# Two encoder layers on one core: earlier DMA slots, past keys turned ahead of the mixer, retention steps regrouped, and a GpSimd power on 128x320 numbers

## What is computed

```python
def _layer(x, l, P, past_k, past_v, s_gla0, s_ret0):
    x = x + 0.5 * _rms_norm(_swiglu(_rms_norm(x, ...), ...), ...)
    m, k_rows, v_rows, s_gla, s_ret = _mixer(_rms_norm(x, ...), ...)
    x = x + _rms_norm(m, ...)
    x = x + 0.5 * _rms_norm(_swiglu(_rms_norm(x, ...), ...), ...)

def _mixer(h, ...):
    z = h @ w_in                                    # low rank, then 26 tiles of 128 columns
    o_a = _rms_norm(_gla_chunked(...)) * silu(gr)    # 4 heads of 64: y tiles 0, 1
    o_d = _rms_norm(_diff_attention(q, [past_k | k], [past_v | v], ...)) * (1 - lam)  # y tiles 2 to 5
    o_r = _layer_norm(_retention_chunked(...)) * silu(rg)    # 4 heads of 64: y tiles 6, 7
    return concatenate([o_a, o_d, o_r]) @ w_out      # norm: y * 1/sqrt(mean(y*y) + eps), per head
```

## Time and profile before

| | us |
|---|---|
| median of 3 runs | 1334.51 (1334.36 to 1334.72) |
| the profiled execution | 1334.34 |
| its span on the core | 1332.6 |
| PE busy | 1315.2 |
| DVE, ACT, POOL busy | 813.3, 634.2, 131.6 |

### The profile page before, as it was taken

How to read it: one execution, slowest core, us unless ns; L and a number is a source line. 1 busy time by engine, 2 the same in 40 slices (tenths; PEclk the granted TensorE clock), 3 DMA queues, 4 the chain that set the end, 5 groups by cost and what they waited for, 6 DMA issues and landing times.

```text
span 1332.6 us, 24615 instructions
## 1 busy us (share of the span) xinstructions
PE 1315.2 (99%) x9508; PEld 1287.2 (97%) x9508; DVE 813.3 (61%) x1263; ACT 634.2 (48%) x1015; POOL 131.6 (10%) x176
## 2 busy tenths in 40 slices
PE   9999999999999999999999999999999999999998
PEld 7999999999999999999999999999999999999998
DVE  6756544687776855554385555437876777556432
ACT  6444434564466644443464443437535575444333
POOL 1000000451010200000030000005500130000000
PEclk9999999999999999999999999999999999999999
DMA  7555554563344454545545544455533355555552
GB/s 210 163 165 161 168 162 144 140 160 93 87 132 127 131 154 143 156 139 151 152 127 146 153 144 146 145 141 160 139 88 90 94 142 169 147 150 147 144 147 66
DMA packets 352027, 187.41 MB, mean 141 GB/s; under 512 B 9016, under 2 KB 348788, under 8 KB 351960
## 3 DMA queue, kind: packets, MB, share of 16 engines
q1 hardware_dynamic: 348376, 177.78, 47.4%
q0 software_dynamic: 2800, 7.85, 1.8%
q10 hardware_dynamic: 784, 0.86, 0.2%
HBM read 180.82 MB, written 4.33 MB: 139 GB/s over the span
## 4 chain that ended last, share of the span: by engine, by line
PE 91%; DVE 4%; POOL 1%; ACT 1%; DVEq 1%; issue 1%; DMA 0%; ACTq 0%; SPq 0%; POOLq 0%
PE ps L716 27%; PE ps L718 26%; PE ps L717 26%; PE ps L745 1%; PE ps L749 1%; PE ps L752 1%; DVE w_l L569 1%; POOL x L577 1%; PE ps L991 1%; PE ps L967 0%; DVEq L1728 0%; PE ps L1076 0%; DVE tiny L1729 0%; PE ps L1055 0%; PE ps L881 0%
## 5 line engine op out<-in xcount | busy, mean ns | idle before, releaser
L716 PE MATMUL ps<-xn_l,w_h 128*128 128x320 f32 x1704 | 536.3, 315 | 2.4 <-DVE w_l L569 2.4
L718 PE MATMUL ps<-xn_h,w_h 128*128 128x320 f32 x1704 | 526.9, 309 | 0.0
L717 PE MATMUL ps<-xn_h,w_l 128*128 128x320 f32 x1704 | 526.8, 309 | 0.0
L569 DVE TENSOR_TENSOR w_l<-raw,w_h 128x1024 fp32r<-128x1024 f32 (+1 forms) x336 | 401.1, 1197 | 158.6 <-ACT w_h L557 158.3
L557 ACT ACTIVATE w_h<-raw 128x1024 fp32r<-128x1024 f32 (+1 forms) x336 | 346.4, 1034 | 210.2 <-DMA raw<-in_ffn_w_down_dram 127.5
L716 PEld LDWEIGHTS ps<-xn_l,w_h 128*128 128x128 f32 x1704 | 321.0, 188 | 6.9 <-issue 3.9
L717 PEld LDWEIGHTS ps<-xn_h,w_l 128*128 128x128 f32 x1704 | 321.0, 188 | 1.0
L718 PEld LDWEIGHTS ps<-xn_h,w_h 128*128 128x128 f32 x1704 | 320.8, 188 | 0.0
L716 PE MATMUL ps<-hid_l,w_h 128*128 128x320 f32 x704 | 217.4, 309 | 0.0
L718 PE MATMUL ps<-hid_h,w_h 128*128 128x320 f32 x704 | 217.4, 309 | 0.0
L717 PE MATMUL ps<-hid_h,w_l 128*128 128x320 f32 x704 | 217.4, 309 | 0.0
(11 more groups left out here) (303 smaller groups left out, 1256.5 us busy)
## 6 DMA issues: line engine op xcount, KB each, us to landing
raw<-in_ffn_w_up_dram SPq DMA_DIRECT2D x172, 512.0 KB, 3.9
raw<-in_ffn_w_down_dram SPq DMA_DIRECT2D x64, 448.0 KB, 3.6
raw<-in_w_in_dram SPq DMA_DIRECT2D x52, 512.0 KB, 3.8
raw<-in_ffn_w_down_dram SPq DMA_DIRECT2D x32, 512.0 KB, 4.0
raw<-in_w_out_dram SPq DMA_DIRECT2D x16, 512.0 KB, 4.1
const<-in_tables_dram POOLq DMA_DIRECT2D x8, 288.0 KB, 4.4
raw<-in_ffn_w_up_dram SPq DMA_DIRECT2D x8, 256.0 KB, 6.6
y<-z SPq DMA_DIRECT2D x16, 80.0 KB, 2.2
```

The source lines that it names most:

```text
L569: dve.tensor_tensor(w_l[s][:, 0:cols], raw[s][:, 0:cols], w_h[s][:, 0:cols], ALU.subtract).then_inc(w_lo, 1)
L716: pe.matmul(out, w_h[s][:, w], xl, start=first, stop=False)
L717: pe.matmul(out, w_l[s][:, w], xh, start=False, stop=False)
L718: return pe.matmul(out, w_h[s][:, w], xh, start=False, stop=last)
```

## The change

1. `first_step` reports the slot of blocks k-1 and k used after each odd k, not all four at the end. The sum of squares of x is multiplied ahead of tiles 4 and 5, not between them. On DVE `other_params` and `lambda_sums` come two steps later.
2. The past keys have a buffer of their own in the upper half of `xn_l`, are loaded by POOL after the last up tile, turned on PE in the border in place of two of the four fillers, and copied by ACT after its squares. DVE waits for the turn before `xn_l` block 4. The step `past` is gone from the schedule.
3. The low-rank tile and the next one are multiplied together for blocks 4 to 7: all that needs `xn_h` first, then all that needs `xn_l`.
4. `ret_o 1` and `ret_mu 1` are each moved ahead of the attention steps of their place; the squares of y tiles 0, 1, 6 and 7 are a step `squares g` one tile earlier.
5. Group a's root: DVE adds eps (128x320, from PSUM), POOL raises the 128x320 numbers to -0.5, and a new step `halves`, one tile later, splits them on DVE. ACT's Sqrt is gone.
6. The first `spread` writes bank 3, so it waits for ACT's `tok7`, and the second for `att_max10`, not for `att_max11`.

```diff
 def first_step(k):
                 for t in range(OPENING):
                     mm = pe.matmul(ps[:, t, 0:T], w_h[s][:, first_block(t, k)], xn_l[:, k, :], start=False, stop=k == KD - 1)
-                    if k == KD - 1:
-                        mm.then_inc(w_used, 1)
+                if k % 2:
+                    mm.then_inc(w_used, 1)
...
+                pe.wait_ge(x_sum, 1)
+                pe.matmul(ps_stat[:, 0:T], sq_2[:, 0:P], ssum[:, :], start=True, stop=True).then_inc(x_stat, 1)
                 for t in range(OPENING, OPENING + 2):
...
-                        stat_x(0, 0)
...
+            def low_rank_and_next(l, n):
+                rest = range(KD // 2, KD)
+                block = lambda w, t, k: w[slot(l, U_MIX + t)][:, k * P:(k + 1) * P]
+                for k in rest:
+                    pe.wait_ge(xn_hi, (l * 4 + n) * KD + k + 1)
+                    pe.matmul(ps[:, 0, 0:T], block(w_h, 0, k), xn_h[:, k, :], start=False, stop=False)
+                for k in rest:
+                    pe.matmul(ps[:, 1, 0:T], block(w_h, 1, k), xn_h[:, k, :], start=False, stop=False)
+                    pe.matmul(ps[:, 1, 0:T], block(w_l, 1, k), xn_h[:, k, :], start=False, stop=False)
+                for t in range(2):
+                    for k in rest:
+                        if t == 0:
+                            pe.wait_ge(xn_lo, (l * 4 + n) * KD + k + 1)
+                        mm = pe.matmul(ps[:, t, 0:T], block(w_h, t, k), xn_l[:, k, :], start=False, stop=k == KD - 1)
+                    mm.then_inc(w_used, 1)
...
                     spread(l, norm // 2)
-                    keep_busy(4)
+                    if norm == 0:
+                        turn_past_keys(l)
+                        keep_busy(2)
+                    else:
+                        keep_busy(4)
...
-    + [("att_t", 1), ("att_s", 3), ("att_a", 2), ("ret_o", 1)] + P8[18][:1] + [("att_o", 1), ("ret_mu", 0)] + P8[18][1:]
-    + [("att_t", 2), ("att_s", 4), ("att_a", 3), ("ret_mu", 1)] + P8[19][:1] + [("att_o", 2), ("tok", 1)] + P8[19][1:]
+    + [("ret_o", 1), ("att_t", 1), ("att_s", 3), ("att_a", 2)] + P8[18][:1] + [("att_o", 1), ("ret_mu", 0)] + P8[18][1:]
+    + [("ret_mu", 1), ("att_t", 2), ("att_s", 4), ("att_a", 3)] + P8[19][:1] + [("att_o", 2), ("tok", 1)] + P8[19][1:]
...
     + [("att_t", 7), ("att_s", 9), ("att_a", 8), ("stat", "a"), ("root", "a")] + P8[24][:1] + [("att_o", 7), ("tok", 7)] + P8[24][1:]
-    + [("att_t", 8), ("att_s", 10), ("att_a", 9)] + P8[25][:1] + [("att_o", 8), ("squares", "b")] + P8[25][1:]
+    + [("att_t", 8), ("att_s", 10), ("att_a", 9)] + P8[25][:1] + [("att_o", 8), ("squares", "b"), ("halves", "a")] + P8[25][1:]
...
-                    elif kind == "root" and n != "a":
+                    elif kind == "root":
+                        dst, src = (inv_a, var_a) if n == "a" else (inv_h[:, STAT_OF[n] - 4, :], var_h[:, STAT_OF[n] - 4, :])
                         after(pool, l, "dve", f"var_{n}")
...
+                        power = minus_half[:, 0:1].broadcast_to([P, T]) if n == "a" else minus_half[:, :]
+                        mark("pool", pool.tensor_tensor(dst, src, power, ALU.pow), f"inv_{n}")
...
+                elif kind == "halves":
+                    after(dve, l, "pool", "inv_a")
+                    dve.tensor_copy(inv_2[:, :], inv_a)
```

More of the change, by code:

```diff
@@ L174, in milestones @@
         elif kind == "root":
[L175 to L180, removed]
+            dve.append(f"var_{n}")
+            pool.append(f"inv_{n}")
+        elif kind == "halves":
+            dve.append("inv_2")
         elif kind == "gates":
@@ L191 @@
 READER = {"tok": ("act", "tok"), "ret_kt": ("act", "ret_kt"), "ketok": ("act", "ketok"), "ret_s": ("dve", "ret_s"),
-          "ret_state": ("dve", "ret_state"), "ret_o": ("dve", "ret_o"), "ret_mu": ("dve", "ret_xc"), "stat": ("act", "sqrt_")}
+          "ret_state": ("dve", "ret_state"), "ret_o": ("dve", "ret_o"), "ret_mu": ("dve", "ret_xc"), "stat": ("dve", "var_")}
 SHARED = [(kind, "" if not arg else arg[0]) for kind, *arg in SCHEDULE
@@ L656, in _ @@
                 pool.memset(near[:, :, :], 0.0)
+                after(pool, l, "pe", "kct1")
+                then_pass(pool)
+                for b, t in ((0, 0), (1, 64), (2, 0)):
+                    i = pool.memset(scores[:, :, b, t:t + 64], 0.0)
+                i.then_inc(mem_set, 1)
                 for kind, *arg in SCHEDULE:
                     n = arg[0] if arg else None
[L659 to L665, removed]
+                    if kind == "weight":
                         qk(l, n)
@@ L718, in product @@
                 return pe.matmul(out, w_h[s][:, w], xh, start=False, stop=last)
-            def low_rank_part(s, bank, k0, k1):
-                for k in range(k0, k1):
-                    w = w_h[s][:, k * P:(k + 1) * P]
-                    pe.matmul(ps[:, bank, 0:T], w, xn_l[:, k, :], start=k == 0, stop=False)
-                    mm = pe.matmul(ps[:, bank, 0:T], w, xn_h[:, k, :], start=False, stop=k == KD - 1)
-                if k1 == KD:
-                    mm.then_inc(w_used, 1)
             def tile_part(s, bank, k0, k1, order=range(KD), xh=xn_h, xl=xn_l):
@@ L759, in opening @@
                     opening_step(l, u0, n, i)
-                for t in range(OPENING):
+                if u0 == U_MIX:
+                    low_rank_and_next(l, n)
+                for t in range(2 if u0 == U_MIX else 0, OPENING):
                     if t == OPENING - 1:
@@ L845, in ffn, with turn_past_keys @@
                     spread(l, norm // 2)
-                    keep_busy(4)
+                    if norm == 0:
[3 more added lines that the diff above has]
+                        keep_busy(4)
+            def turn_past_keys(l):
+                pe.wait_ge(past_keys_in, (l + 1) * 16)
+                for n in range(2):
+                    for h in range(H):
+                        mm = pe.transpose(ps_m[:, n, h * P:(h + 1) * P], kc_raw[:, n, h * P:(h + 1) * P], C("ident"))
+                    mark("pe", mm, f"kct{n}")
             def turned(t, banks, k0, k1, done):
@@ L951, in mixer_step @@
                 bank3 = ps[:, 3, :]
[L952 to L958 removed]
+                if kind == "logit":
                     pe.wait_ge(evac, l * GROUPS + G_MIX + 1)
@@ L1082, in mixer_step @@
                     elif n == "b":
-                        after(pe, l, "dve", "head2")
+                        after(pe, l, "dve", "att_max11")
                     else:
@@ L1198, in pre, with past_keys @@
                     hi(act, l, u0 + v)
+                if n == 1:
+                    past_keys(l)
                 act.preload_act_table(ACT.Sqrt)
                 root_x(l, m)
+            def past_keys(l):
+                for n in range(2):
+                    after(act, l, "pe", f"kct{n}")
+                    mark("act", act.activation(kc_t[:, :, n * P:(n + 1) * P], ps_m[:, n, :].rearrange("p (h c) -> p h c", h=H),
+                                               ACT.Copy), f"kct{n}")
             def y_tile(l, m, i, phase, bank, b, gain, used):
@@ L1278, in mixer_step @@
                 rows3 = bank3[:, 0:3 * P].rearrange("p (i c) -> p i c", i=3)
-                if kind == "past":
-                    after(act, l, "pe", f"kct{n}")
-                    mark("act", act.activation(kc_t[:, :, n * P:(n + 1) * P], ps_m[:, n, :].rearrange("p (h c) -> p h c", h=H),
-                                               ACT.Copy), f"kct{n}")
-                elif kind == "tok":
+                if kind == "tok":
                     dst = dk_tok[:, :, n, :] if n < 4 else dv_tok[:, :, n - 4, :] if n < 8 else \
@@ L1377, in mixer_step @@
                     mark("act", i, f"squares_{n}")
-                elif kind == "root":
-                    if n == "a":
-                        after(act, l, "pe", "ms_a")
-                        mark("act", act.activation(root_a, bank3[:, 0:T], ACT.Sqrt, bias=C("eps")), "sqrt_a")
                 elif kind == "gates":
@@ L1526, in post @@
                 for k in range(KD):
+                    if n == 1 and k == KD // 2:
+                        after(dve, l, "pe", "kct1")
                     split_lo(l, n, k, x, norm, k)
```

91 lines of the change are left out of this document (39 added, 52 removed).

## The result

The changed kernel took 1410.05 us (median; 1409.81 to 1413.24) against 1334.43 of the kernel before on the same chip: 1.0572 times as long (95% interval 1.0554 to 1.059), a loss of 75.6 us. The forecast was 1518.4. The direction was right, and the time lies in the range, but inside the span of rival B (1336 to 1434); the loss was put at 184 us, 2.4 times what it is.

The account below looks back on a forecast made before the run. PE was taken to bound the kernel, busy 1315.2 of 1332.6 us. From 1334.34 us, 10.1 gained (3.9 + 1.7 + 0.9 + 2.2 + 1.4) and 194.2 lost to the power gave 1518.4; range 1340 to 1556.

Parts of the forecast that it names:

- rival B: Group a's power on POOL is mostly setup or an unfilled loop: 11 to 60 us, time 1336 to 1434; chance 0.21.
- The power: Group a's inverse root on POOL: 102 us a layer, of which PE loses 97, or 194 in both.
- W: Time of POOL's 128x320 power in a layer, put at 102 us, with 9.9 us of it hidden from PE.
- Case C: A power of 320 costs little more than one of 3, under 10 us: 1322.8 us in all; chance 0.18.
- The catch-up: After PE's wait for the power: 2.9 us for DVE's queue and 1.9 for the low clock, each layer.
- The old wait for `att_max11`: PE's wait before the spread: no gain under a long power; 0.7 us a layer gained in Case C.
- The start: Edits around tile 4: 3.9 us gained, 2.4 from PE's wait for low weights and 1.5 from the half clock.
- Keys: Past keys' transposes moved into the border in place of fillers: 0.87 us a layer gained, 1.7 in all.
- Opening: New matmul order for blocks 4 to 7, fewer waits for `xn_l`: 0.45 us a layer gained, 0.9 in all.
- Retention: PE's four waits for DVE's `ret_o` copy and the subtraction after `ret_mu 1`: 2.2 us gained in all.
- the statistics' wait: PE's wait of 0.53 us before group a's statistics goes: 0.7 us a layer with overlap, 1.4 in all.
- A: The power costs by the number, 0.32 us each: the forecast of 1518.4 us; chance 0.58.

Follow-up runs that it names:

- 88 numbers: The changed kernel with only 88 of group a's 320 numbers raised to the power on POOL, the rest multiplied: 1337.12 us.
- the power alone: The kernel before with only group a's root changed (eps on DVE, power on POOL, halves one tile later): 1424.58 us.
- the late reciprocal: The changed kernel with group a's root as a Sqrt on ACT from PSUM and the DVE reciprocal one tile later, at the halves: 1332.1 us.
- the Sqrt from SBUF: The changed kernel with eps on DVE, group a's Sqrt on ACT out of SBUF, and the reciprocal one tile later, no power: 1330.35 us.

## Why the prediction was wrong in size

**The power, the term that failed.** The step that failed is the split of the 1.127 us of a 128x3 power: the prediction took 0.17 us of it as fixed, from a memset, and put the other 0.96 to three numbers, 0.32 us each. The runs show 0.160 us a number, so 0.48 of the 1.127 belong to the numbers and 0.65 do not grow with them. W was 51.36 instead of 102. This alone is 2 x 50.6 = 101 us of the miss of 108. The choice was argued with "nothing in the trace hints at" a setup; the trace did not speak against one either, and two of the three rival cases rested on one. The measured W is in rival B's span of 11 to 60, and B's ground, that most of the time of three numbers is not theirs, is what came. Case C, with W under 10, is off on the other side: an addition of 128x320 takes 1.09 us, the power took 51.36.

**With W = 51.36 the prediction's own sum is 1334.34 - 10.1 + 2 x 46.26 = 1416.8**, against 1410.05. The 6.8 us left are:

- *The catch-up*, 4.8 us a layer in the sum, was 2.57: 4.5 us too much in all. Of it about 1.6 are the low clock (11 distances between starts at 0.266 instead of 0.147 are 1.3, and the two spread matmuls take 0.3 longer), forecast 1.9. So 1.0 is left for the backlog of DVE, not 2.9, and most of that is not the power's: the kernel with the multiplication has 4.54 in this stretch too, 0.75 more than before, with PE waiting 0.7 for `probs_t`. With 88 numbers it is 6.36, as with 320, so it does not grow with the power. I had taken nearly all of DVE's 3.8 us of queue as a loss. That PE at half clock gives DVE time to catch up, so that the two terms hide each other, would explain it; no run tells them apart.
- *A wait counted wrong.* "The old wait for `att_max11` gives no gain, since PE stands for the power there": but I had already set it off when I found that PE reaches the spread at 390.1, and never credited its 0.7. The spread comes 55.84 us after the statistics; by my own times it is 380.2 + 51.36 - (376.37 - 0.73) = 55.9. The sum had 0.7 a layer more, 1.5 in all. The experiment with the power alone shows the same wait from the other side: there it costs 2.3 a layer.
- *The start* gained 4.39, forecast 3.9 (0.5). Its 1.5 for the clock came out by luck: it had nothing for the parameters on DVE, and where the clock stayed up with these at their old place, a wait of 1.54 stood in its place.

**The gains.** Keys: 0.90 from the low-rank step to the state, forecast 0.87. Opening: 0.41, forecast 0.45. Retention and the statistics' wait: 1.93, forecast 1.1 + 0.73. The half clock at 36 us is gone, as forecast (1.00 in each us from 20 to 60). All of them together are seen in the kernel in which the power is a multiplication (1323.04 against 1322.8) and in the one with the Sqrt, which leaves nothing out (1323.93).

**What was hidden.** PE's wait was to be W - 9.9 = 41.5; it is 41.37. That DVE's idle time is nearly as long, that the clock falls with it, and that the stores behind the power cost nothing (no wait in the trace names them) came as forecast.

**The chances.** A had 0.58 and B 0.21. From a single long row of three numbers, setup and slope can't be told apart; the two should have had like chances, and the likeliest time should have been taken between the ends.

## What to carry to other kernels

A duration at one small size is a point, not a line: before an operation is made a hundred times larger, measure it at two sizes in an engine's idle time, which cost here no more than 1 us. Work off the critical path is free only up to what hides it, here 10 us; beyond that it cost W - 7 to W - 8 us a layer here, and with 320 numbers no engine but POOL worked for 36 us, so put the reader late and let nothing urgent stand behind it. An inverse root of 128x320 belongs here on ACT and DVE (2.15 us for the reciprocal; 1323.93 us, against 1410.05 with the power), at a point where DVE is waiting anyway (one tile later it was 1332.1), and a power on POOL only for as many numbers as the wait hides: here 40 cost nothing, and 88 cost 7.0 us a layer. And when a wait is taken away, look what stands next in the queue: the gain of the start needed a third edit that nobody had priced.

## What the runs showed of the hardware

- POOL's power of 8 to 320 fp32 numbers in a partition took 0.160 us a number and 0.2 to 1.2 us besides: 51.36 us for 128x320, 47 times the addition's 1.09. Below eight numbers it was uneven: 0.68, 1.20, 1.21 and 1.01 us for one to four, one measurement each.
- While PE stood idle the granted clock fell from 1.00 to 0.50, the lower of the two levels that the trace shows (2805 of its 2810 stretches of 0.5 us are at one of them), and stayed there for 4 and 5 us after it had restarted, and for 9 and 4 us in the kernel with the power alone. After the stop of 41 us in layer 0 that cost only 1.6 us.
- With the late reciprocal PE waited 1.6 us for `probs`, and for less just around it, in both layers. The half clock came behind it in layer 1 (0.50 from 1043 to 1049 us), and in layer 0 of the same execution it did not (1.00 from 384 to 400); with the Sqrt from SBUF it came in both. Behind the wait of 2.4 us at the start it came in the kernel before (0.50 from 36.30 to 39.70), and not in the one with the power alone (1.00 from 35 to 44).
